# Encoder layer on one core: a ranking unit, the prompt's q/k transposes and the attentions' output projections change places

## The reference

```python
def encoder_layer(x, mem, ...):
    h = rmsnorm(x, norm_mix_g)
    q, k, v, z_sg, gate_logits = jnp.split(h @ w_in, IN_SPLITS, axis=-1)      # 1024, 256, 256, 2048, 2048 wide
    q = apply_axial_rope(rmsnorm(q, q_norm_g)); k = apply_axial_rope(rmsnorm(k, k_norm_g))
    attn_branch = block_attention(q, k, v) @ w_attn_o                          # 16 heads of 64, 4 kv heads
    sg_branch = spatial_gating(gelu(z_sg), sg_norm_g, sg_w, sg_b) @ w_sg_o
    g_attn, g_sg = jnp.split(sigmoid(gate_logits), 2, axis=-1)
    x = x + (g_attn * attn_branch + g_sg * sg_branch) @ w_out
    x = x + cross_attention(rmsnorm(x, norm_xa_g), rmsnorm(mem, norm_mem_g), wq_xa, wkv_xa, wo_xa)
    x = x + peer_ffn(rmsnorm(x, norm_ffn_g), w_peer_q, peer_k1, peer_k2, expert_down, expert_up)
    return x
# peer_ffn: per token and each of 8 heads, scores against 2 x 128 sub-keys, top 16 of each, top 16 of the
# 256 sums, softmax; then sum over the chosen experts of gate * gelu(down[e] . x) * up[e]
y_prompt, y_sample = rmsnorm(xp, final_norm_g), rmsnorm(xs, final_norm_g)
```

## Time and profile before

| what | value |
|---|---|
| median of three runs | 2602.77 us |
| span of the profiled execution | 2596.5 us |
| PE busy | 2453.0 us, 94% |
| DVE busy | 2168.5 us, 84% |
| POOL busy | 1369.1 us, 53% |
| ACT busy | 1097.1 us, 42% |
| mean DMA rate | 303 GB/s |

### The profile page before, as it was taken

The page is one execution under the profiler, slowest core; times in us unless marked ns, Lnnn a source line. Parts: engine busy times, 40 slices in busy tenths (PEclk is TensorE's granted clock), DMA queues, the critical chain, the costliest instruction groups (busy, mean ns, idle before and its releaser), DMA issues.

```text
span 2596.5 us, 38792 instructions
## 1 busy us (share of the span) xinstructions
PE 2453.0 (94%) x13143; PEld 2072.0 (80%) x13143; DVE 2168.5 (84%) x3950; ACT 1097.1 (42%) x1939; POOL 1369.1 (53%) x1054
## 2 busy tenths in 40 slices
PE   7988999899999999999998889999999999999998
PEld 5767888788876778877876667888888888888987
DVE  6355445886679797877899978999999999999999
ACT  4463444343247313443317993333333333343333
POOL 0000000315742464655665547788788877777875
PEclk9999999999999999999999999999999999999999
DMA  6745545447973788877953559999999999999998
GB/s 249 269 136 178 195 146 178 177 186 270 382 272 114 281 313 320 323 280 259 364 177 135 210 227 402 408 412 415 415 412 415 415 413 415 415 415 400 414 415 310
DMA packets 240423, 787.52 MB, mean 303 GB/s; under 512 B 21904, under 2 KB 75328, under 8 KB 219552
## 3 DMA queue, kind: packets, MB, share of 16 engines
q0 software_dynamic: 112288, 408.77, 40.3%
q1 hardware_dynamic: 128000, 377.00, 39.0%
HBM read 728.01 MB, written 57.67 MB: 303 GB/s over the span
## 4 chain that ended last, share of the span: by engine, by line
PE 33%; DVE 28%; issue 17%; ACT 9%; DMA 8%; POOL 4%; DVEq 1%; POOLq 0%; SPq 0%; ACTq 0%
PE lin L245 9%; PE lin L247 9%; PE lin L246 9%; DVE Y L2454 4%; ACT row_ring L1826 4%; DMA w_raw<-in_up,now 2%; DVE low L2431 2%; DVE w_raw L2440 2%; DVE w_lo L222 2%; DVE low L2420 2%; DVE rows L2440 2%; DVE row_ring L138 2%; PE tr L1755 2%; DMA rows<-in_up,now 2%; DVE gl L2464 1%
## 5 line engine op out<-in xcount | busy, mean ns | idle before, releaser
L150 POOL DMA_INDIRECT row_ring<-in_down,IDX x256 | 365.4, 1428 | 314.2 <-DVE dots L138 241.2
L222 DVE TENSOR_TENSOR w_lo<-w_raw,w_hi 128x2048 fp32r<-128x2048 f32 x100 | 230.1, 2301 | 227.5 <-ACT w_hi L214 213.5
L245 PE MATMUL lin<-w_hi,T_hi 128*128 128x512 f32 x976 | 389.2, 399 | 15.6 <-DVE w_lo L222 7.2
L247 PE MATMUL lin<-w_hi,T_lo 128*128 128x512 f32 x976 | 388.4, 398 | 0.0
L246 PE MATMUL lin<-w_lo,T_hi 128*128 128x512 f32 x976 | 385.9, 395 | 0.0
L214 ACT ACTIVATE w_hi<-w_raw 128x2048 fp32r<-128x2048 f32 x116 | 221.8, 1913 | 351.7 <-PE lin L247 334.4
L2313 POOL DMA_INDIRECT rows<-in_up,now x192 | 309.0, 1609 | 64.7 <-issue 53.9
L138 DVE CUSTOM_DVE_ANT_0 row_ring<-row_ring,H 128x1024 f32<-128x1024 f32 x256 | 302.9, 1225 | 33.6 <-DMA row_ring<-in_down,IDX 32.9
L245 PE MATMUL lin<-w_hi,c_hi 128*128 128x512 f32 x768 | 307.1, 400 | 17.5 <-DVE c_lo L2467 17.3
L2313 POOL DMA_INDIRECT w_raw<-in_up,now x189 | 277.6, 1469 | 84.3 <-issue 43.8
L245 PE MATMUL tr<-T_hi,w_hi 128*128 128x384 f32 x896 | 303.6, 339 | 2.2 <-DVE low L2420 2.2
(11 more groups left out here) (305 smaller groups left out, 5255.2 us busy)
## 6 DMA issues: line engine op xcount, KB each, us to landing
w_raw<-in_wall SPq DMA_DIRECT2D x116, 1024.0 KB
row_ring<-in_up SPq DMA_DIRECT2D x128, 512.0 KB
G<-in_downT SPq DMA_DIRECT2D x112, 512.0 KB
wd<-dense_gates SPq DMA_DIRECT2D x32, 768.0 KB
weight_rests<-w_lo SPq DMA_DIRECT2D x16, 1024.0 KB, 4.9
w_lo<-weight_rests SPq DMA_DIRECT2D x16, 1024.0 KB
dense_gates<-peer SPq DMA_DIRECT2D x6, 2048.0 KB, 6.7
dense_gates<-w_raw SPq DMA_DIRECT2D x5, 2048.0 KB, 6.9
```

Source lines behind the costliest of these rows:

```text
L150: pool.indirect_dma_start(self.ring[:, r % self.K, :], None, self.table, bass.IndirectOffsetOnAxis(ap=self.IDX[:, r:r + 1], axis=0)).then_ ...
L222: dve.tensor_tensor(self.lo[:, h % 2], self.raw[:, h % 2], self.hi[:, h % 2].bitcast(F32), ALU.subtract).then_inc(self.lo_done, 1)
L245: pe.matmul(out, lhs[0], rhs[0], start=start, stop=False, skip_group_check=True)
L247: return pe.matmul(out, lhs[1], rhs[0], start=False, stop=stop, skip_group_check=True)
```

## The change

Three places move; no arithmetic is added or removed.

- `rank(2)` leaves `routing` (where the last chunk now only splits its two weight halves) and runs in the sample's `mixer_inputs` on DVE, behind `turn.dve` and ahead of the wait for the tables. Unit 3 moves from (0,0) to (1,0) and unit 4 from (1,0) to (2,0). POOL's program is not changed.
- In the prompt's `mixer_inputs` the transposes of q/k tile 0 follow both tiles' matmuls of half 0, and those of tile 1 follow both tiles' matmuls of half 1. ACT copies them accordingly: the split of the next half comes ahead of the first copy, and the second copy stands behind the squares. The sample keeps its places.
- The output projections no longer wait for all blocks. `Blocks.upto` waits before row block k for `out_lo` of k + 1. In self-attention two tiles' half 0 (`first_half`, 12 matmuls each) is also issued within the draining steps N + 1 and N + 2.

```diff
+class Blocks:
+    def upto(self, pe, kk, bank):
+        if kk + 1 > self.seen:
+            pe.wait_ge(self.out_lo, kk + 1)
+            self.seen = kk + 1
+def first_half(pe, st, h, T, t, last_tile, lin, blocks):
+    st.wait(pe, h)
+    for k in range(HK):
+        cols = slice(t * P, (t + 1) * P)
+        blocks.upto(pe, k, t)
+        last = three(pe, lin[:, t, :], (T[0][:, k, cols], T[1][:, k, cols]),
+                     (st.hi[:, h % 2, k, :], st.lo[:, h % 2, k, :]), start=(k == 0), stop=False)
+    if t == last_tile:
+        last.then_inc(st.used, 1)
...
+        TURN_AT = [(0, 1), (1, 1)] if NT == 2 else [(0, t) for t in range(NT)]
...
-            def between(c, i):
-                if 1 <= c <= 3:
-                    qk_turn((c - 1) * NT + i)
+            def between(c, half, i):
+                if 1 <= c <= 3 and (half, i) in TURN_AT:
+                    qk_turn((c - 1) * NT + TURN_AT.index((half, i)))
...
-                if 1 <= c <= 3:
+                if 1 <= c <= 3 and NT == 4:
                     for t in range(NT):
                         copy((c - 1) * NT + t)
                 st.split_hi(act, H + 2 * c + 2)
+                if 1 <= c <= 3 and NT == 2:
+                    copy((c - 1) * NT)
...
+                if 1 <= c <= 3 and NT == 2:
+                    copy((c - 1) * NT + 1)
                 wait_odd(act, 2 * c + 3)
...
             if q.first:
                 st.split_lo(dve, 1)
+            else:
+                choice.rank(dve, choice.HERE - 1)
             dve.wait_ge(small_in, 64)
...
-                    r = {(0, 0): 3, (1, 0): 4, (3, 0): 5, (3, 1): 6, (4, 0): 7, (4, 1): 8}.get((c, half))
+                    r = {(1, 0): 3, (2, 0): 4, (3, 0): 5, (3, 1): 6, (4, 0): 7, (4, 1): 8}.get((c, half))
...
+                if step > N:
+                    first_half(pe, st, q.h0 + 2 * W_AO, T, step - N - 1, q.nt - 1, lin, blocks)
                 if 2 <= step < N + 2:
                     turn(step - 2)
...
-            attended(pe)
-            project_tokens(pe, st, H, 2, T, range(NT), lin, o)
+            project_tokens(pe, st, H, 2, T, range(NT), lin, o, turn=blocks, begun=2)
...
-            attended(pe)
-            project_tokens(pe, st, H0, 2, T, range(NT), lin, o_x)
+            project_tokens(pe, st, H0, 2, T, range(NT), lin, o_x, turn=blocks)
...
-                if c >= 1:
+                if 1 <= c < NPC - 1:
                     choice.rank(dve, c - 1, lambda: st.split_lo(dve, H0 + 7 + 2 * c))
                 else:
                     st.split_lo(dve, H0 + 7 + 2 * c)
```

More of the change, by code:

```diff
@@ L263, in project_tokens @@
             for i, t in enumerate(tiles):
+                if half == c == 0 and i < begun:
+                    continue
                 bank = n * (c % sets) + i
@@ L280, in project_tokens @@
                     last.then_inc(st.used, 1)
-                if half == 0 and between is not None:
-                    between(c, i)
+                if between is not None:
+                    between(c, half, i)
 def project_features(pe, st, h0, nchunks, T, groups, lin, o, between=None, turn=None):
@@ L1010, in self_attention @@
         block_end = [(hp + 1) * q.nt for hp in range(NH // 2)]
+        blocks = Blocks(out_lo)
         @block.tensor
```

26 lines of the change are left out of this document (14 added, 12 removed).

## The result

The changed kernel took 2608.92 us (median of 20 runs, 2603.00 to 2616.12) against 2600.28 us for the kernel before (20 runs, 2593.91 to 2609.44). The ratio is 1.0036 [1.0027, 1.0045], in brackets its 95% interval: slower by 0.36%, some 9 us. The ratios are estimated from all runs and differ a little from the quotient of the medians (1.0033 here). The forecast was 2597.6 us, with a range of 2590 to 2604.5. It started from the median of three runs, 2602.77; the twenty lie 2.5 us lower.

What follows compares the result with a forecast made beforehand. PE was busy 94% of the span, leaving idle time at seams to win. Terms +0.7 - 1.8 - 1.2 - 0.2 - 2.7 + 0 = -5.2 us gave span 2591.3, plus 6.3 the median 2597.6 us; range 2590 to 2604.5.

Steps and rivals of the forecast that it cites:

- The merged gap: Prompt's q/k transposes: PE's waits of 1.78 and 1.53 us become one of about 3.4 us before half 1.
- the one in chunk 3 is hidden, because the next `w_lo` is late by its load: Prompt's q/k transposes: chunk 3's slow-clock stretch costs nothing; the next wait shrinks from 2.76 to about 1 us.
- with that wait short, the slow stretch at 83 goes: -1.5: Prompt's q/k transposes: the existing 1.2 GHz stretch from 83 to 86 us disappears, gaining 1.5 us.
- Rival 4: Prompt's q/k transposes: slow clock behind all three merged gaps, the 83 us stretch stays; +4.5, total 2601.4 us; chance 0.08.
- DVE's gather rows behind it hold the next split at its old place, near 878: Sample's self-attention end: after the last block, DVE's next weight split stays near 878; PE needs it at 883.7.
- the 5.7 us of the forecast: Sample's self-attention end: the last block is made 5.7 us later, but half 1 needs it only 3.7 us after that.
- I take 2.7, nearer to no wait, since before the change none stood in this stage: Sample's self-attention end: gain of 2.7 us, bounds 0.4 and 3.7, depending on gathered rows being there in time.
- Gain 0; bounds -2.0 (all kept) and +1.0 (a longer stretch at the lower clock): Sample's cross-attention end: PE starts 2.0 us earlier, then waits as much longer for `G`, 4.9 us; no net change.
- Rival 2: Sample's ranking unit: tables land late, DVE waits for `small_in`; at 8.2 us landing +4.8, total 2607.6 us; chance 0.10.
- The two waits of the working: Sample's ranking unit: PE waits about 4.1 us for `qn`, DVE idles 9.9 us before the tables.
- sum of -5.2: Whole kernel: all places together make it 5.2 us faster, 0.2%, likeliest verdict no change; chance 0.52.

Runs made afterwards that it cites:

- The filler: Kernel before with the prompt's q/k transposes moved and filler matmuls (1.8, 3.1, 3.1 us) on PE ahead of half 1; ratio 0.9988.
- five moved rows: Kernel before with block-wise waits and early tiles in both self-attentions, five of the sample's gathered rows on DVE moved ahead of the last `T_lo`; ratio 0.9993.

## Why the prediction was wrong

**The prompt's q/k transposes: +0.7 said, +4.2 measured.** The merged gap, its length and the lower clock behind it were right. The failing step is "the one in chunk 3 is hidden, because the next `w_lo` is late by its load" and "with that wait short, the slow stretch at 83 goes: -1.5". It took the landing of the loads as fixed. But a load is issued when DVE has split the slot's last content, so it moves with the chain that the slow clock delays. The merged gap in chunk 1 brought no lower clock, which alone would have put the sum 0.7 us lower; the one in chunk 3 did, and was not hidden. SP's queue issues the two loads of that chunk at 67.99 and 71.27 us before and at 69.20 and 71.40 after:

```profile
69.20 0.43 SPq L205 DMA_DIRECT2D w_raw<-in_wall  x1
...
71.40 0.82 SPq L205 DMA_DIRECT2D w_raw<-in_wall  x1
```

From 60 to 70 us the DMA engines moved 186 GB/s (245 before), and from 70 to 80 they were full in both. What is missing in the first is 10 us x 59 GB/s = 0.59 MB; the 0.12 MB that they had moved more from 50 to 60 (252 against 240 GB/s) leave 0.47 MB, 1.4 us of their full rate of 341 GB/s in the next window. This is an estimate. ACT's copy of the second load starts 1.5 us later than before (83.86 against 82.37), its next ones wait for loads too, and so comes the new gap at 96.30:

```profile
92.00 1.92 ACT L214 ACTIVATE w_hi<-w_raw 128x2048 fp32r<-128x2048 f32 x1 [3.60 <-DMA w_raw<-in_wall]
99.33 1.92 ACT L214 ACTIVATE w_hi<-w_raw 128x2048 fp32r<-128x2048 f32 x1 [5.41 <-DMA w_raw<-in_wall]
```

The copy at 92.00 stood at 89.75 before, and the gap brings the stretch at 1.2 GHz that I had struck off. Rival 4 had this part at +4.5 and was nearest, partly by luck: it had a slow stretch in all three chunks and the one at 83 us kept, where two chunks and a new one at 96 us were the case. Its total of 2601.4 was far off, since it had the ends as forecast. The filler shows that the clock started it; the accounting by bytes in flight is worked out from the windows, not isolated by a run. The rule of the Trainium skill ("TensorE: Matmul & The Clock Gate", "HAM oscillation — how this bites in real kernels"), that a burst behind a long enough wait starts at the lower clock, each time again, was the better guide here: the trace agrees at gaps of 3.53, 3.53 and 2.30 us. It did not come at the gap of 2.31 us at 35.69.

**The end of the sample's self-attention: -2.7 said, +5.8 measured.** This is the largest error. The failing step is "DVE's gather rows behind it hold the next split at its old place, near 878". I had counted the last block 5.7 us late, found that PE needs it only later, and did not add up DVE's queue: 870.93 + 0.6 + nine rows of 1.15 us is 881.9, where the split indeed starts. Even the 5.7 us of the forecast, 868.2 + 0.6 + 10.3 = 879.1, would have been late. Before, DVE had 4.8 us of slack there; the change used 6.9 (the 8.4 us less the 1.5 by which the stage itself starts later). The second step, "I take 2.7, nearer to no wait, since before the change none stood in this stage", failed too: a gathered row cost 3.5 us, because POOL's requests stand behind its wait for all blocks. It took the slack in which DVE could have caught up. Both went with the early tiles or with five moved rows, always together, so that their shares stay open. What no term of the sum had at all is the lower clock behind PE's wait for `G`, 2.7 us.

**The end of the sample's cross-attention: 0 said, +3.2 measured,** above the bound of +1.0. The mechanism was named (DVE's gathered rows, PE then waits longer for `G`), but the failing step is "Gain 0; bounds -2.0 (all kept) and +1.0 (a longer stretch at the lower clock)": the price assumed that the rows' requests keep their place. In the kernel with the block-wise waits alone they start 3.4 us later for the trace's own shift and 3.0 more: PE's earlier start brings the split forward to where the casts are, and they take 3.04 and 1.39 us for 1.04 and 0.40. The longer stretch at the lower clock, the bound that I had named, is the small part: 6.18 us for the 32 transposes against 5.38 before, 0.8 us. PE's wait for `G` is 6.33 us where I had 4.9.

**The ranking unit: -0.2 said, 0 measured.** The two waits of the working came out, 4.0 and 9.9 us against 4.1 and 9.9; whether the sum is -0.2 or 0 can't be told here. Rival 2 had named the right place, but the tables landed 2.6 us after the last of the four was issued, as in the forecast.

**The prompt's ends: -1.8 and -1.2 said, -2.1 and -1.9 measured.** Right, with the second some 0.7 us too small, and kept to the end. PE waits 2.86 us for `G` before the prompt's gating matmuls (1.00 before) without losing the gain.

So the sum of -5.2 became +9.2 by three places, +3.5, +8.5 and +3.2 us off. In all three an engine that I had taken as having slack, or a transfer that I had taken as fixed in time, moved with the edit.

## What to carry over

Work slipped into a drain is paid by whatever is queued behind the last result on the engine that waits for it: add up that queue, compare it with the slack that it had, and move it ahead of the wait before the drain is lengthened. Two short waits merged into one are not equal to it, since the clock may fall behind the longer one, as it did here; fill it or leave the two. A wait that grows costs again by the lower clock behind it (2.7 us behind one of 4.3 at the sample's self-attention). And when a stage's end comes earlier, the small transfers and requests that one engine issues in order (tables, gathered rows) have to be moved with it. Here that gave the largest gains: 4.2 us at the tables and, together with the block-wise wait, 4.2 at the gathered rows.

## What the runs showed of the hardware

- The granted clock fell to 0.50, 1.2 GHz, behind gaps of 3.5 us (four of four, in the changed kernel and in that with the q/k transposes alone), and also behind one of 2.30 us at 96.30 and one of 2.02 us at 96.00, but not behind one of 2.31 us at 35.69 (1.00 from there to 41 us). Behind those it was low from the first matmul. In the kernel before it fell about 1 us into the work behind the gap of 2.76 us at 81.82, and 1.5 us into that behind the gap of 2.00 us at 863.24 (matmuls of 0.39 us took 0.63 from 864.8 on). The length of the gap alone does not decide in this range.
- POOL's cast of 128x1024 to bf16 took 1.04 us beside an idle DVE and 3.04 us when it began 0.16 us into DVE's weight split of 2.29 us: it ended 0.9 us after the split did. In the changed kernel it began 0.4 us into a split, took 2.79 us and ended 0.9 us after it too. I read this as a cast held up for the split and then run at its usual speed. That agrees with the Trainium skill ("SBUF — State Buffer", "SBUF: two separate sides"), which says that a GpSimd operation and a DVE operation with two inputs in SBUF take turns on one port pair, each for its whole length.
- The last stage, the same program in all kernels, differed by up to 9 us between executions, and single stretches that no edit touched by up to 5 us. A part of 2 us can't be read from one pair of traces; over a dozen kernels it can, to about 1 us.
